# Nine dense stages of a two-model kernel: each in its own block, or consecutive ones as parts of one block

## The reference

```
# first block, its end
hf = rms_norm(x, ffn_pre_norm) * (1 + sc_f) + sh_f
f = (silu(hf @ w_ffn_gate) * (hf @ w_ffn_up)) @ w_ffn_down      # 1024 -> 2816 -> 1024   "ffn1"
x = x + g_f * rms_norm(f, ffn_post_norm)
# second block
for layer in (0, 1):
    h = h + 0.5 * swiglu(rms_norm(h), ...)                      # "ffn2", "ffn4"
    hn = rms_norm(h)
    h = h + (pool_fox_mixer(hn) if layer == 0 else mla_mixer(hn))
                    # end in a product with w_out (1024 x 1024): "ab_out", "mla_out";
                    # mla_mixer begins with hn @ w_in (1024 x 416): "mlain"
    h = h + 0.5 * swiglu(rms_norm(h), ...)                      # "ffn3", "ffn5"
return rms_norm(h)                                              # "finish"
```

## Time and profile before

| | us |
|---|---|
| median of 3 executions | 2938.02 |
| lowest, highest | 2934.63, 2939.4 |
| the profiled execution, own time | 2938.13 |
| its span, first to last instruction | 2936.3 |
| mean granted TensorE clock | 0.966 of 2.4 GHz |
| TensorE busy | 2751.4 (94%) |
| VectorE, ScalarE, GpSimd busy | 1340.2, 831.6, 561.9 |

### The profile page before, as it was taken

One profiled execution on the slowest core, in us unless ns is written; L12 is line 12 of the kernel. 1 busy time (PEld: TensorE's weight loads), 2 busy tenths in 40 slices (PEclk: granted clock), 3 DMA queues, 4 the chain that ended last, 5 costly groups with the idle time before them and its releaser, 6 DMA issues. The chain is left out here.

```text
span 2936.3 us, 39084 instructions
## 1 busy us (share of the span) xinstructions
PE 2751.4 (94%) x16394; PEld 2178.4 (74%) x16394; DVE 1340.2 (46%) x1879; ACT 831.6 (28%) x1240; POOL 561.9 (19%) x383
## 2 busy tenths in 40 slices
PE   6989897869999799999988999999999999899998
PEld 4768855658888678887766888878888746688887
DVE  3454668353232543434455434344343556543433
ACT  2232135232122322213243212132122336321222
POOL 2000123132021220312301212022121200121302
PEclk7999989979999999999999999999999999999999
DMA  7250210112322232223302233233232230223321
GB/s 254 72 161 31 90 39 1 58 55 88 101 93 80 72 100 92 95 94 84 100 16 86 90 97 101 90 97 100 90 98 90 61 101 1 76 97 101 100 80 51
DMA packets 256943, 248.26 MB, mean 85 GB/s; under 512 B 25972, under 2 KB 252088, under 8 KB 256640
## 3 DMA queue, kind: packets, MB, share of 16 engines
q1 hardware_dynamic: 256562, 245.70, 26.7%
q10 hardware_dynamic: 206, 0.06, 0.0%
HBM read 241.52 MB, written 2.12 MB: 83 GB/s over the span
## 5 line engine op out<-in xcount | busy, mean ns | idle before, releaser
L383 DVE TENSOR_TENSOR ffn_wt_lo<-ring,ffn_wt_hi 128x2048 fp32r<-128x2048 f32 (+1 forms) x166 | 413.8, 2493 | 258.9 <-ACT ffn_wt_hi L368 258.9
L368 ACT CAST ffn_wt_hi<-ring 128x2048 fp32r<-128x2048 f32 (+1 forms) x166 | 307.6, 1853 | 771.9 <-PE bank L561 771.9
L1060 POOL TENSOR_TENSOR ffn_act_hi<-ffn_act,const 128x512 fp32r<-128x512 f32 x110 | 216.9, 1972 | 1324.8 <-DVE ffn_act L1051 1324.8
L561 PE MATMUL bank<-feat_hi,ffn_wt_hi 128*128 128x512 f32 x1056 | 331.8, 396 | 19.0 <-DVE feat_lo L442 10.5
L561 PE MATMUL bank<-feat_lo,ffn_wt_hi 128*128 128x512 f32 x1056 | 329.1, 393 | 0.0
L561 PE MATMUL bank<-feat_hi,ffn_wt_lo 128*128 128x512 f32 x1056 | 329.1, 393 | 0.0
L561 PE MATMUL bank<-ffn_act_hi,ffn_wt_hi 128*128 128x512 f32 x880 | 271.6, 390 | 0.9 <-POOL ffn_act_lo L1062 0.9
L561 PE MATMUL bank<-ffn_act_hi,ffn_wt_lo 128*128 128x512 f32 x880 | 271.0, 389 | 0.0
L561 PE MATMUL bank<-ffn_act_lo,ffn_wt_hi 128*128 128x512 f32 x880 | 271.0, 389 | 0.0
L561 PEld LDWEIGHTS bank<-feat_hi,ffn_wt_hi 128*128 128x128 f32 x1056 | 198.8, 189 | 67.6 <-issue 10.6
L561 PEld LDWEIGHTS bank<-feat_lo,ffn_wt_hi 128*128 128x128 f32 x1056 | 199.4, 189 | 44.0
(11 more groups left out here) (601 smaller groups left out, 4286.1 us busy)
## 6 DMA issues: line engine op xcount, KB each, us to landing
ring<-in_ffn_w_gate SPq DMA_DIRECT2D x44, 1024.0 KB, 5.3
ring<-in_ffn_w_up SPq DMA_DIRECT2D x44, 1024.0 KB, 5.3
ring<-in_ffn_w_down SPq DMA_DIRECT2D x32, 1024.0 KB, 5.1
ring<-in_ada_w SPq DMA_DIRECT2D x24, 1024.0 KB, 7.3
ring<-in_ffn_w_down SPq DMA_DIRECT2D x16, 768.0 KB, 4.4
ring<-in_w_ffn_gate SPq DMA_DIRECT2D x11, 1024.0 KB, 5.3
ring<-in_w_ffn_up SPq DMA_DIRECT2D x11, 1024.0 KB, 5.3
ring<-in_w_in SPq DMA_DIRECT2D x8, 1024.0 KB, 5.4
```

The costliest lines, as they stand in the source:

```text
L368: self.nc.scalar.copy(self.wh[:, n % 2, 0:words], K.ring[:, n % RING, 0:words]).then_inc(K.high_done, 1)
L383: self.nc.vector.tensor_tensor(self.wl[:, n % 2, 0:words], K.ring[:, n % RING, 0:words], self.wh[:, n % 2, 0:words].bitcast(F32), ALU.subt ...
L561: lasts[m] = pe.matmul(outs[m], a, b, start=n == 0 and p == 0, stop=end and p == 2)
L1060: nc.gpsimd.tensor_tensor(ah[:, f, :], a[:, i % 2, :], K.k("ones")[:, 0:1].broadcast_to([P, T]), ALU.mult)
```

## The change

A `Section` holds the tiles `wt_hi`, `wt_lo`, `act_hi`, `act_lo`, `silu`, `act` and runs a list of parts in one block: each engine runs the first part's instructions, then the second's, with no barrier between. Each part still has its own small tiles and semaphores. There are three sections: ffn1, ffn2; ab_out, ffn3, ffn4, mlain; mla_out, ffn5, finish. A part's tail casts and subtracts the first chunk of the part that follows, in one piece; where ffn has its last down chunk and ab_out and mla_out their last chunk, this stands ahead of the evacuation of their last tiles in both queues. The features of ffn1 go into `K.fh`, `K.fl`, those of ab_out and mla_out into the section's `act_hi`, `act_lo`. Borrowed tiles: mlain's small ones lie in `silu` and `act`, the post-norm's squares in the MLA tiles, finish's output in `K.h`. Where the barrier stood, waits on semaphores stand now:

```diff
 class Ahead
-            K.nc.vector.scalar_tensor_tensor(K.fl[:, k, :], ..., ALU.subtract)
+            K.nc.vector.scalar_tensor_tensor(K.fl[:, k, :], ..., ALU.subtract).then_inc(self.s_lo, 1)
...
     def add(self, pool):
-            pool.drain()
+            if k < self.DONE - 1:
+                pool.drain()
+            else:
+                pool.drain().then_inc(self.s_acc, 1)
 class PostNorm
-    def squares(self, act):
+    def squares(self, act, prev):
+        act.wait_ge(prev.s_acc, 1)
         for m in range(2):
+            act.wait_ge(prev.done[0], prev.done[1] - 1 + m)
             K.nc.scalar.activation(self.sq[m], K.h[:, KD - 2 + m, :], ACT.Square).then_inc(self.s_sq, 1)
 class Split
-        self.pieces = K.plan.segments[first]["n0"] if defer else None
-        if defer:
+        self.prev = sec.parts[-1] if sec.parts else None
+        self.pieces = K.plan.segments[first]["n0"] if defer and not self.prev else None
+        if defer or norm and sec.act:
             self.hh, self.hl = K.fh, K.fl
+        elif sec.act:
+            self.hh, self.hl = sec.act[:2]
-        self.wh, self.wl = st.sb("wt_hi", ...), st.sb("wt_lo", ...)
+        self.wh, self.wl = sec.wh, sec.wl
     def features_scalar
             for k in range(Ahead.DONE, KD):
+                if self.prev:
+                    act.wait_ge(self.prev.done[0], self.prev.done[1] - KD + k + 1)
                 self.nc.scalar.mul(self.hh[:, k, :], K.x[:, k, :], self.defer(k)).then_inc(self.s_hh, 1)
     def features_deferred
         dve.wait_ge(self.s_sq, 2)
+        if self.prev:
+            dve.wait_ge(self.prev.ahead.s_acc, 1)
     def features_vector
-            first_low(dve)
+            if not self.prev:
+                first_low(dve)
     def feature
-            if k >= self.made:
+            if k < self.made:
+                if self.prev:
+                    pe.wait_ge(self.prev.ahead.s_lo, k + 1)
+            else:
                 pe.wait_ge(self.s_hl2 if k % 2 else self.s_hl, (k - self.made) // 2 + 1)
+class Section:
+    def run(self):
+        with self.st, self.K.nc.Block() as block:
+            @block.sync
+            def _(sp):
+                for part in self.parts:
+                    part.sync(sp)
...
 ffn_stage, now ffn_part; scalar (vector: the same with low)
-                S.high(act, name, 0)
+        if self.lead:
+            S.high(act, name, 0)
...
                 elif c < end - 1 and c + 1 not in early:
                     S.high(act, name, c + 1, words(c + 1))
+                elif c == end - 1 and self.follow:
+                    S.high(act, *self.follow)
 linear_stage, now linear_part; evacuate
                 if n + 1 < len(chunks):
                     split(e, a, b, w)
+            elif self.follow:
+                split(e, *self.follow)
 finish_stage, now finish_part
+            act.wait_ge(prev.done[0], prev.done[1] - KD + k + 1)
             nc.scalar.activation(K.h[:, k, :], K.x[:, k, :], ACT.Square).then_inc(s_sq, 1)
...
+        pe.wait_ge(prev.ahead.s_hh, Ahead.DONE)
         for n in range(4):
             turn(n, range(0, 4)).then_inc(s_t, 1)
+        pe.wait_ge(*prev.done)
 mla_in_stage, now mla_in_part
+        box["free"] = prev.hidden_read
     def sync(sp):
+        sp.wait_ge(*box["free"])
         sp.dma_start(box["pos_i"][:, :], io["positions_2"][0].partition_broadcast(P)).then_inc(box["pos"], 16)
```

More of the change, by code:

```diff
@@ L1073, in linear_stage @@
[L1073 removed]
+    st = sec.part(name)
+    S = Split(K, sec, st, name, norm, defer, post)
+    ah, al, g, a = sec.act
+    s_gate, s_silu, s_act, s_al, s_free, s_sq, s_acc = st.sems("gate_scaled", "silu", "act", "act_low", "out_read", "out_squared", "squares_added")
+    early = (1, 2) if post else (1,)
+    nxt = Ahead(K, st, ahead, exact) if ahead else None
+    thirds = [(t, 12 * t, 8 * t, steps) for t, steps in enumerate(THIRDS)]
@@ new lines, in linear_part @@
+    st = sec.part(name)
+    S = Split(K, sec, st, tiles[0][0], norm, defer)
+    s_v, s_s = st.sems("vector_out", "scalar_out")
+    nxt = Ahead(K, st, ahead) if ahead else None
+    mine = [scalar(t) for t in range(len(tiles))]
+    if "sems" in extra:
+        extra["sems"](st)
+    if "box" in extra:
+        extra["box"]["read"], extra["box"]["split"] = s_v, S
+    chunks = []
+    for t, (seg, j, _, _, _, _, _, words) in enumerate(tiles):
+        if not chunks or chunks[-1][:2] != (seg, j):
+            chunks.append((seg, j, words, []))
+        chunks[-1][3].append(t)
@@ new lines, in sync, with tensor @@
+    def sync(sp):
+        if "sync" in extra:
+            extra["sync"](sp)
+        K.stream(sp, plan.end(tiles[-1][0]) + RING)
+    def tensor(pe):
+        S.sums(pe)
+        for seg, j, _, members in chunks:
+            w = S.chunk(pe, seg, j, tiles[members[0]][3])
+            for t in members:
+                at("at_tensor", t)
+                shape = tiles[t][5]
+                if t >= banks:
+                    o = t - banks
+                    pe.wait_ge(s_s if mine[o] else s_v, sum(x == mine[o] for x in mine[:o + 1]))
+                product3(pe, K.bank[t % banks][0:shape[0], 0:shape[1]], tiles[t][4](S, pe, w, t == 0)).then_inc(K.tiles_done, 1)
+        if "tensor" in extra:
+            extra["tensor"](pe)
@@ new lines, in gpsimd, with linear_stage @@
+    def gpsimd(pool):
+        S.features_pool(pool, src)
+        if "pool" in extra:
+            extra["pool"](pool)
+        if nxt:
+            nxt.add(pool)
+    self = Bag()
+    self.first, self.done, self.ahead = chunks[0][:3], (s_v, mine.count(False)), nxt
+    self.sync, self.tensor, self.scalar, self.vector, self.gpsimd = sync, tensor, scalar_side, vector, gpsimd
+    sec.add(self)
+def linear_stage(K, name, *args, **kwargs):
+    sec = Section(K, name)
+    linear_part(K, sec, name + "_", *args, **kwargs)
+    sec.run()
```

649 lines of the change are left out of this document (316 added, 333 removed).

## The result

| | before | after |
|---|---|---|
| median | 2938.71 | 2905.51 |
| lowest, highest | 2934.63, 2944.0 | 2903.8, 2909.84 |
| profiled execution, own time | 2938.13 | 2904.97 |
| its span | 2936.3 | 2903.1 |

A forecast was written before the change was run, and what follows sets the result against it. TensorE, busy 94% of the span, was taken as the bound. Terms 14.4 + 6.0 - 0.85 + 1.9 + 0.5 + 13.4 = 35.3 us off 2938.13 gave 2902.8, said as 2903, range 2897 to 2918.

The forecast's parts named there:

- Waits for the first weights: Ahead of ffn3, ffn4, mlain and ffn5: TensorE no longer waits for the first chunk's split, 14.4 us won.
- Low clock: Behind those four waits: the 1.2 GHz clock after idle time goes, four times 1.5 us, 6.0 us won.
- The moved split costs nothing: Tail of the part ahead: splitting the next part's chunk 0 there costs nothing, with cover of 2.8 us.
- The exception, mlain: At mlain's head: single tiles make the sum wanted earlier, so TensorE stands about 0.85 us, subtracted from the gain.
- the thinnest cover: In mlain: VectorE's split of mla_kv is ready at 2339.7 and wanted at 2340.1, a cover of 0.4 us.
- Norm chain, finish: ffn1 to ffn2 and ffn5 to finish: squares start earlier without the barrier, 1.9 us and 0.5 us won.
- The address: Gate and up chunks of ffn1 and ffn2: weights no longer 32 bytes off a multiple of 64, 13.4 us won.
- The clearing of semaphores ... between 0 and 1 us: Nothing at barriers; at the kernel's end 30 more semaphores cleared together cost between 0 and 1 us.
- A: Rival: the slow rate has another cause and ffn1 and ffn2 stay slow; 2916, chance 0.13.
- B: Rival: covers at the borders don't hold or the clock still falls, half of 21.9 given back; 2914, chance 0.13.
- C: Rival: the slow rate spreads to the other parts' gate, up and down matmuls; 2955, chance 0.04.
- D: Rival: only the other three parts' gate and up chunks turn slow, ffn1 and ffn2 stay slow; 2937, chance 0.04.

The follow-up runs named there:

- b1_aligned: The kernel before with a tile of 32 bytes per partition added ahead of the weight tiles in ffn1 and ffn2; 2939.0, ratio 1.0003.
- r1_after: The kernel after run again unchanged, for its time and one more profile; 2907.02, ratio 0.9894.
- experiments 6: The kernel after with every part splitting its own first chunk whole at its head and no split in the tail; 2935.47, ratio 0.9991.
- experiment 7: The kernel after without the tail split, each deferred part splitting its own first chunk at its head in four pieces; 2922.64, ratio 0.9947.
- b2_layouts: The kernel before with gaps of several sizes between features, weights and hidden tiles, different in each feed-forward part; 2962.93 in its one execution.
- experiment 9: The kernel after with 3.6 us of idle VectorE work ahead of feature 6 in ffn3, ffn4, mlain and ffn5; 2908.62, ratio 0.9897.
- experiment 10: The kernel after with GpSimd clearing mla_out's and ffn5's semaphores inside finish; 2901.51, ratio 0.9875, and 2901.99 when run again.
- experiments 3 and 4: The kernel after with a 32-byte tile ahead of the first section's weights, 2921.63; the kernel before with small tiles of ffn1 and ffn2 behind large ones, 2926.13.

## Why the prediction was right

The total was right, 2905.5 for 2903, and the terms that the prediction named are right one by one, but for the clearing. Outside its working stand three terms, which the table above shows: 5.2 us lost in abin, fox and ab_out, 2.7 won ahead of ffn1, and 1.2 won in the mla stages. That these come to only 1.3 us together is luck. With the first goes the granted clock, as shown above. The second is an execution's own: b1_aligned, with the old code there, gained 1.65 at the same point (first matmul of ffn1 at 623.75 instead of 625.40), and r1_after lost 2.2 (627.59). In the third the stretch from mlain to the mla attention took 1.4 us less at a mean granted clock of 0.93 for 0.91; nothing more was tried on it.

- **Waits for the first weights.** Right to 0.1 us, read from the earlier trace rows; experiments 6 and 7 put them back.
- **Low clock.** 6.0 predicted from ffn3's first twelve matmuls, 6.6 measured up to the sum. The mechanism was right for this pair of traces. What the prediction didn't see is that the low clock is not certain: it did not follow the idle times of 1.76 us in experiment 7, nor one of 2.85 us ahead of mlain in b2_layouts, and it did follow one of 2.85 us at abin's head after the change, where 1.1 us went that the sum has at nothing.
- **The moved split costs nothing.** Right; the covers were wider than said. What the step left out was the idle time of VectorE behind ab_out and mla_out, of 2.2 us, which experiment 9 filled without loss.
- **The exception, mlain.** The stall was 0.41 and not 0.85, since the chain to the sum took 4.9 us from the last tile and not the 5.4 that I added up from the earlier trace rows. The mechanism was right, as the 3.0 us of experiment 9 show, which all fall here. mla_kv, called the thinnest cover with 0.4 us, had 1.0: split at 2315.6, wanted at 2316.6.
- **Norm chain, finish.** 2.2 and 0.6 for 1.9 and 0.5, right.
- **The address.** The size (13.4) and the bounds were right, and the forecast was made for the layout whose rate the trace showed, which is why it held. The reason given, "the weights begin 32 bytes off a multiple of 64", failed: 64 and 4160 are slow as well. What sorts all the phases tried is the distance between moving tile and weight tile: whole multiples of 256 bytes were fast, all others slow. With the reason as it was, a pad of 32 bytes would have looked like the same gain and brought nothing (experiment 1). The two pages of the Trainium skill that spoke against it ("TensorE: Matmul & The Clock Gate", Step-by-step, and "SBUF — State Buffer", SBUF: two separate sides) would have left ffn1 at 89.60 us; it ran at 87.04. The measurement decides: the rate hangs on the distance between the two tiles that TensorE reads. Why, no run here shows.
- **"The clearing of semaphores ... between 0 and 1 us".** This step failed in size: the end took 2.4 us more, and 2.0 of them came back when the clearing of 30 semaphores was moved away from it (experiment 10). The gaps at barriers were the wrong rows for it, since they show what other engines wait for between two blocks, and behind the last one no other engine has work that GpSimd's could run beside. I read a cost that may have been hidden there as no cost; how much clearing costs between blocks was not tried.
- **Rivals.** A was half right: the rate has another cause than the one I read, but its forecast, that ffn1 and ffn2 stay slow, is refuted by the thirds of 87.04 us and by experiments 3 and 4. B (no cover, or a clock that still falls) is refuted by experiment 9 and by the four heads after the change, C and D by the thirds of ffn3, ffn4 and ffn5 at 87.04 and 43.52 us.

## What to carry to other kernels

Lay out the tiles that one matmul reads at distances of whole multiples of 256 bytes per partition, and put small tiles behind the large ones: here that alone brought 12 us of 2938, without one instruction changed. Between stages that follow each other the barrier was the small part here (7 us of 23) and the first weights' preparation the large one (16): prepare them in the tail of the stage ahead, ahead of its last evacuation. Put the cleaning up of a kernel's end under its last transfers, which gave back 2.0 us here. And when two traces are compared, look first at the stretches that the change doesn't touch: here they differed by up to 5 us through the clock.

## What was not expected of the hardware

- A stream of 512-column fp32r matmuls starts every 0.2267 us or every 0.2289 to 0.2343 us (a third divided by its 384 or 192 matmuls), by the distance of its two tiles alone.
- The length of the idle time did not decide the clock behind it. Behind 1.76 us it was 1.00 (ffn4 and mlain in experiment 7). Behind 2.85 us it was 0.50 ahead of ffn4 and mlain in the kernel before (11.15 us from ffn4's first matmul to its sum against 9.67), and 1.00 ahead of mlain in b2_layouts and ahead of abin in the kernel before.
- The same instructions with the same busy time met a clock of 1.00 in one kernel and 0.50 in another, and each kernel did so in both of its profiles, 2.6 us in fox and 1.6 in ab_out.
- The end of the kernel took 2.4 us more with 30 more semaphores to clear, and 2.0 less when they were cleared earlier, though GpSimd's part of it shows in no busy row.
